# Mixer projections: step-size columns multiplied together with the gate columns, and the column copy divided between two engines

## What is computed

```python
cut = np.cumsum(IN_SPLITS)[:-1].tolist()   # pool, z, xbc, dt (12), qkv (1152), gate (384), a (12), b (12)
pc = jnp.split(h_ctx @ w_in, cut, axis=-1)
pl = jnp.split(h_lat @ w_in, cut, axis=-1)
s_lat, _, _ = ssd_stream(pl[1], pl[2], pl[3], *ssd_p, ssd_sf, ssd_sb)
g_lat, _, _ = gdn_stream(to_column_major(pl[4]), to_column_major(pl[5]), to_column_major(pl[6]),
                         to_column_major(pl[7]), *gdn_p, gdn_sf, gdn_sb)
# ssd_stream: dt = softplus(dt_raw + dt_bias);  gdn_stream: g = -exp(a_log) * softplus(a_raw + dt_bias), beta = sigmoid(b_raw)
```

## Time and profile before

| | |
|---|---|
| median of 3 runs | 4005.32 us (4003.27 to 4006.92) |
| span of the profiled execution | 4003.8 us |
| TensorE busy | 3512.2 us, 88% |
| VectorE, ScalarE, GpSimd busy | 47%, 27%, 31% |
| the stage in2 | from about 2418.7 to 2700 us of the span |

### The profile page before, as it was taken

How to read it: one execution, slowest core, us unless ns; L and a number is a source line. 1 busy time by engine, 2 the same in 40 slices (tenths; PEclk the granted TensorE clock), 3 DMA queues, 4 the chain that set the end, 5 groups by cost and what they waited for, 6 DMA issues and landing times. The chain is left out here.

```text
span 4003.8 us, 48185 instructions
## 1 busy us (share of the span) xinstructions
PE 3512.2 (88%) x16881; PEld 2311.3 (58%) x16881; DVE 1895.7 (47%) x4073; ACT 1088.2 (27%) x2218; POOL 1253.6 (31%) x1004
## 2 busy tenths in 40 slices
PE   8999997998898999999995898998867776949996
PEld 3745776676445667667565447574457764524442
DVE  2046662553663566766873450425479485240011
ACT  1023333442332232433442440221114112111111
POOL 2211010433333555655663452002212553211110
PEclk9999998999998999999998996998988877969998
DMA  4255532322541121112114423123325713347986
GB/s 133 92 165 143 163 120 79 107 84 101 203 148 32 58 65 56 46 55 65 52 43 156 163 111 84 42 71 104 115 78 157 255 51 125 119 173 253 325 313 230
DMA packets 417236, 494.07 MB, mean 123 GB/s; under 512 B 70786, under 2 KB 320922, under 8 KB 417011
## 3 DMA queue, kind: packets, MB, share of 16 engines
q1 hardware_dynamic: 391559, 463.71, 34.9%
q0 software_dynamic: 4608, 16.78, 1.6%
q10 hardware_dynamic: 20844, 10.68, 0.9%
HBM read 362.32 MB, written 128.77 MB: 123 GB/s over the span
## 5 line engine op out<-in xcount | busy, mean ns | idle before, releaser
L1067 POOL TENSOR_TENSOR hgrn_queries<-hgrn_qd,hgrn_pair_decay 128x640 f32<-128x640 f32 x192 | 263.2, 1390 | 293.3 <-PE hgrn_ps_a L1182 253.5
L1117 PE MATMUL hgrn_ps_w<-xT,hgrn_ring 128*128 128x512 f32 x432 | 196.0, 600 | 1.8 <-PEq L34 1.8
L396 PE MATMUL gla_bg_ps<-gla_bg_w,xT 128*128 128x256 f32 x768 | 186.0, 386 | 5.8 <-DMA gla_bg_w<-in_w_in_ab_dram 5.8
L530 POOL TENSOR_TENSOR l_wsum<-l_ring 128x512 f32<-128x512 f32 x14 | 20.0, 1430 | 507.9 <-PE att_bg_ps L562 187.2
L1721 PE MATMUL end_ps_z<-end_w,end_yT 128*128 128x512 f32 x384 | 166.9, 594 | 1.4 <-ACT end_yT L1668 1.4
L2843 PE MATMUL end_ps_z<-end_w,end_yT 128*128 128x512 f32 x384 | 167.3, 595 | 0.8 <-ACT end_yT L2771 0.8
L396 PEld LDWEIGHTS gla_bg_ps<-gla_bg_w,xT 128*128 128x128 f32 x768 | 144.4, 193 | 36.5 <-issue 10.6
L1287 DVE TENSOR_TENSOR hgrn_k_end<-hgrn_kd,hgrn_end_decay 128x128 f32<-128x128 f32 x168 | 136.0, 848 | 9.0 <-issue 2.2
L1117 PEld LDWEIGHTS hgrn_ps_w<-xT,hgrn_ring 128*128 128x128 f32 x432 | 81.6, 193 | 94.1 <-issue 93.8
L1117 PE MATMUL hgrn_ps_w<-hgrn_xs,hgrn_wsum 128*128 128x512 f32 x288 | 130.5, 601 | 4.6 <-ACT hgrn_sig L1401 4.6
L2162 ACT ACTIVATE att_s_sb<-att_s_sb,att_shift 128x256 f32<-128x256 f32 (+1 forms) x192 | 88.9, 464 | 166.3 <-DVE att_shift L2119 166.2
(11 more groups left out here) (681 smaller groups left out, 7861.5 us busy)
## 6 DMA issues: line engine op xcount, KB each, us to landing
expw_wg<-in_exp_w_gate_dram SPq DMA_DIRECT2D x16, 2048.0 KB, 10.1
expw_wu<-in_exp_w_up_dram SPq DMA_DIRECT2D x16, 2048.0 KB, 16.3
expw_wd<-in_exp_w_down_dram SPq DMA_DIRECT2D x16, 2048.0 KB, 21.9
att_w_ada<-in_ada_w_dram SPq DMA_DIRECT2D x24, 1024.0 KB, 6.8
hgrn_ring<-in_w_in_c_dram SPq DMA_DIRECT2D x18, 1024.0 KB, 5.4
l_ring<-in_w_in_ab_dram SPq DMA_DIRECT2D x14, 1024.0 KB, 5.7
end_gt<-gate_l SPq DMA_DIRECT2D x16, 768.0 KB, 8.6
hgrn_ring<-in_w_in_c_dram SPq DMA_DIRECT2D x24, 512.0 KB, 5.6
```

Of the source, the lines that this page charges most:

```text
L396: last = pe.matmul(bank[0:job.rows, q * job.width:(q + 1) * job.width], job.acts[:, k, t * P:t * P + job.rows], w[:, k, 0:job.width], star ...
L1067: pool.tensor_tensor(queries[:, d, s, :].rearrange("p (b a c) -> p b a c", b=POINTS, a=PC), q, f, ALU.mult).then_inc(queries_done, 1)
L1117: last = pe.matmul(bank[:, :], a[:, k, :], x(k), start=(fresh and k == 0), stop=(k == HK - 1), skip_group_check=True)
```

## The change

The 12 step-size columns lose their own two jobs. A `Job` can now have a second piece of columns `beside` the first, with a weight column and a destination of its own; the two pieces lie side by side in the weight buffer, are multiplied as one width, and are loaded and stored by a DMA each. On the context the step sizes stand beside the 24 columns a and b (width 36), on the latent tokens beside the 216 (width 228, on hT_cols). The lead-in has 5 fills for 7. The latent step sizes now lie in DRAM in column order of the tokens, and `Decays.load` reads them back into raster order, by two DMAs for the latent tokens and one for the context. The waits on loads and stores count the DMAs of the pieces. Of the eight column copies VectorE makes the first five, ahead of its clearing of in_u, and GpSimd the last three.

```diff
-    def __init__(self, kind, acts, tokens, weights, col, width, units, dst):
+    def __init__(self, kind, acts, tokens, weights, col, width, units, dst, beside=None):
         self.kind, self.acts, self.tokens, self.weights = kind, acts, tokens, weights
+        self.pieces = [(0, col, width, dst)]
+        if beside is not None:
+            self.pieces.append((width, *beside))
+            width += beside[1]
...
+        pieces = [len(job.pieces) for job, _ in self.units]
+        self.loads_by = [16 * sum(pieces[u % ring:u + 1:ring]) for u in range(len(self.units))]
+        self.stores_by = [16 * sum(pieces[self.fills[e][0]] for e in range(f % stages, f + 1, stages)) for f in range(len(self.fills))]
...
-        at = job.col + c * job.width
-        sp.dma_start(self.w[u % self.ring][:, :, 0:job.width],
-                     job.weights.rearrange("(k p) n -> p k n", p=P)[:, :, at:at + job.width]).then_inc(self.w_loaded[u % self.ring], 16)
+        for first, col, width, _ in job.pieces:
+            at = col + c * width
+            sp.dma_start(self.w[u % self.ring][:, :, first:first + width],
+                         job.weights.rearrange("(k p) n -> p k n", p=P)[:, :, at:at + width]).then_inc(self.w_loaded[u % self.ring], 16)
...
+            for first, _, width, dst in job.pieces:
+                out = dst[top:top + tall, c * width:(c + 1) * width].rearrange("(q p) c -> p q c", p=job.rows)
+                sp.dma_start(out, rows[:, :, first:first + width]).then_inc(self.stored[f % self.stages], 16)
...
-                    pe.wait_ge(self.w_loaded[u % self.ring], 16 * (u // self.ring + 1))
+                    pe.wait_ge(self.w_loaded[u % self.ring], self.loads_by[u])
...
-            wait(act, self.stored[f % self.stages], 16 * (f // self.stages))
+            wait(act, self.stored[f % self.stages], self.stored_of(f - self.stages))
...
-            sp.dma_start(self.raw[:, :, 0:H], self.dt_raw.rearrange("(t p) c -> p t c", p=P)).then_inc(self.loaded, 16)
+            lat = self.dt_raw[0:SEQ, :].rearrange("(w t b) c -> b w t c", t=TILES, b=2)
+            for b in range(2):
+                sp.dma_start(self.raw[b * GRID_W:(b + 1) * GRID_W, 0:TILES, 0:H], lat[b]).then_inc(self.loaded, 16)
+            sp.dma_start(self.raw[:, TILES:T2, 0:H], self.dt_raw[SEQ:ROWS2, :].rearrange("(t p) c -> p t c", p=P)).then_inc(self.loaded, 16)
...
-        dve.wait_ge(self.loaded, 112)
+        dve.wait_ge(self.loaded, 144)
...
+        BY_DVE = 5
...
+        def turn_columns(eng, k):
+            eng.tensor_copy(by_columns[:, k, :].rearrange("p (w r) -> p r w", r=GRID_H),
+                            by_rows[:, k, :].rearrange("p (r w) -> p r w", w=GRID_W)).then_inc(in_columns, 1)
+
         @block.gpsimd
         def _(pool):
-            for k in range(KB):
-                pool.tensor_copy(by_columns[:, k, :].rearrange("p (w r) -> p r w", r=GRID_H),
-                                 by_rows[:, k, :].rearrange("p (r w) -> p r w", w=GRID_W)).then_inc(in_columns, 1)
+            for k in range(BY_DVE, KB):
+                turn_columns(pool, k)
...
         def _(dve):
+            for k in range(BY_DVE):
+                turn_columns(dve, k)
             conv.clear(dve)
...
-                        Job(TOKEN, hcT, CTX, w, dt_at, DT_WIDTH, 1, dt_raw[con, :]),
-                        Job(TOKEN, hcT, CTX, w, ab_at, 2 * DT_WIDTH, 1, gate_ab[con, Z_WIDTH:GATE_AB]),
-                        Job(TOKEN, hT, SEQ, w, dt_at, DT_WIDTH, 1, dt_raw[lat, :]),
-                        Job(TOKEN, hT_cols, SEQ, w, gate_at + first, GATE_AB - first, 1, gate_ab[lat, first:GATE_AB]),
+                        Job(TOKEN, hcT, CTX, w, ab_at, 2 * DT_WIDTH, 1, gate_ab[con, Z_WIDTH:GATE_AB], (dt_at, DT_WIDTH, dt_raw[con, :])),
+                        Job(TOKEN, hT_cols, SEQ, w, gate_at + first, GATE_AB - first, 1, gate_ab[lat, first:GATE_AB], (dt_at, DT_WIDTH, dt_raw[lat, :])),
```

More of the change, by code:

```diff
@@ L349, in store @@
         else:
-            first, tall = n * job.per * job.rows, job.per * job.rows
-            out = job.dst[first:first + tall, c * job.width:(c + 1) * job.width].rearrange("(q p) c -> p q c", p=job.rows)
-            sp.dma_start(out, src[0:job.rows, 0:job.per * job.width].rearrange("p (q c) -> p q c", c=job.width)).then_inc(self.stored[f % self.stages], 16)
+            top, tall = n * job.per * job.rows, job.per * job.rows
+            rows = src[0:job.rows, 0:job.per * job.width].rearrange("p (q c) -> p q c", c=job.width)
+            for first, _, width, dst in job.pieces:
+                out = dst[top:top + tall, c * width:(c + 1) * width].rearrange("(q p) c -> p q c", p=job.rows)
+                sp.dma_start(out, rows[:, :, first:first + width]).then_inc(self.stored[f % self.stages], 16)
     def begin(self, sp):
@@ L375, in end, with stored_of, all_stored @@
             self.transfer(sp, g)
-        for b in range(self.stages):
-            sp.wait_ge(self.stored[b], 16 * len(range(b, len(self.fills), self.stages)))
+        self.all_stored(sp, len(self.fills))
+    def stored_of(self, f):
+        return 0 if f < 0 else self.stores_by[f]
+    def all_stored(self, sp, fills):
+        for f in range(max(0, fills - self.stages), fills):
+            sp.wait_ge(self.stored[f % self.stages], self.stored_of(f))
     def multiply(self, pe, g):
@@ L3093, in sigmoid @@
     def sigmoid(self, act):
-        act.wait_ge(self.loaded, 112)
+        act.wait_ge(self.loaded, 144)
         act.activation(self.beta[:, :, :], self.b_raw[:, :, :], ACT.Sigmoid)
@@ L3169, in _ @@
             bg.put(sp, LEAD + 1)
-            for b in range(bg.stages):
-                sp.wait_ge(bg.stored[b], 16 * len(range(b, LEAD, bg.stages)))
+            bg.all_stored(sp, LEAD)
             decays.load(sp)
```

## The result

In the first comparison the changed kernel took 3972.5 us (median of four runs, 3967.8 to 3983.3), the kernel before 4006.1 (four runs, 4003.3 to 4020.6). The ratio measured is 0.9901, with a 95% interval from 0.9876 to 0.9927; it is not the quotient of these two medians, which is 0.9916. Five more rounds of both kernels give 0.9921, from 0.9908 to 0.9935. The profiled execution of the changed kernel has a span of 3966.0 us for 4003.8. To tell what the change itself brought, the stage is read first.

A forecast was written before the change was run, and what follows sets the result against it. TensorE, 88% busy, was taken to bound the kernel. The lead-in sums to 1.0 + 6.8 + 1.3 + 26.7 = 35.8 us for 65.7, saving 29.9: span 3973.9, median 3975.4 us, range 3970 to 3984.5.

The forecast's parts named there:

- Steps 1 and 2: Lead-in: 160 narrow records removed, 34.1 us; the kept context fill, 36 columns wide, takes 6.8 us.
- Step 3: Lead-in start: the first fill needs two loads, so TensorE starts 1.0 us later (0.6 to 1.3).
- Step 4: Wide fills at 228 columns: 192.6 ns a record, 24.7 us, plus half the low-clock time; 26.7 us (26.2 to 27.2).
- Step 5: Column copies, five on VectorE and three on GpSimd, one after the other: TensorE waits 1.3 us (0 to 6.0).
- Steps 6 to 8: Lead-in: wide-fill weights hidden by 2 us, in_w by 17 us; extra stores and later decay loads cost nothing.
- Sum: Lead-in 35.8 us for 65.7, saving 29.9; everything behind moves with it; median 3975.4 us, bounds 3973.2 to 3980.9.
- Chances: Forecast and its bounds 0.80; faster 0.94, same 0.04, slower 0.02; range 3970 to 3984.5 us, including the spread of the runs.
- A: Rival: clock rises already in the narrow work, wide fills start at 2.4 GHz; 3.4 us more saved, 3972.0 us; chance 0.06.
- B: Rival: weights of the wide fills become the bound, TensorE waits 10 us; 21.0 us saved, 3984.3 us; chance 0.08.
- C: Rival: a later wait takes nearly all of the lead-in's gain, total within 0.2%; chance 0.04.
- D: Rival: late decay loads of latent step sizes delay ScalarE's sigmoid and stop TensorE; slower than before; chance 0.02.

The follow-up runs named there:

- the parts alone: Against the kernel before: only the context step sizes merged, copies shared, stage 62.2 us for 68.0; only the latent step sizes merged, 41.9 us.

## Why the prediction was right and where it was wrong

**Steps 1 and 2 (removed, context fill).** Right: 213 ns a record at 36 columns, and the parts alone brought 5.8 and 26.1 us.

**Step 3 (later start).** 1.0 us forecast; 3.36 us behind the first issue for 2.34: 1.0.

**Step 4 (wide fills).** 192.6 ns a record forecast, 192.5 seen. The time at low clock was set at 4 us from 3.0 to 4.9. The two traces of the changed kernel have 3.0 and about 5.3 us, the one with all copies on GpSimd about 4.4, and the one with the context fill last 5.7. The middle was right, the upper bound a little short.

**Step 5 (copies).** The mechanism was right, the size was off. The engines do take turns, and VectorE's copies were held as the row with 1.76 us had it. But the price of a copy was 0.91 us and not the 1.2 us that I took with its gap. The nearest row, a strided copy of the same shape at 1130 ns, was a tenth longer than the 1014 ns seen here, and in a row the copies have no gap but overlap by some 0.1 us. The copies ended 10.1 us behind the start for 11.4, and the wait was 0 for 1.3 us; that they ended 0.06 us ahead of TensorE is luck, since nothing in the sum made the two meet. The page "SBUF — State Buffer" of the Trainium skill (section "SBUF: two separate sides") has an exclusive lock on a shared port pair, held for a whole instruction. The shared copies agree with it: VectorE's copies beside GpSimd's were 2.62 to 2.75 us from start to start, for 1.77 + 0.91 = 2.68. The Trainium skill's page "VectorE: DVE Perf Modes" (section "Mode 2×_2P") has two elements a cycle for such a copy, by my estimate some 0.6 us. The runs do not show that: 0.91 us a copy is, by an estimate with the 0.96 GHz that this page of the Trainium skill gives, 1.2 elements a cycle.

**Steps 6 to 8.** Nothing waited for the weights of the wide fills, for stores or for the loads of the decays. The weights' two pieces landed at 2422.8 and 2423.4, 2.9 us before TensorE came to them, where 2 us were forecast. The last load of the decays was issued at 2463.1 and ScalarE's sigmoid came at 2488.8.

**The sum.** 29.9 us forecast for the stage, 31.8 and 30.7 seen in two traces of the changed kernel. Of the difference 1.3 us are step 5; the low clock of step 4 took 0.5 us less than forecast in the first trace and 0.6 us more in the second.

**The range.** This failed, and with it the forecast of the total. By the ratio of the first comparison the kernel is at 3965.7 us, 4.3 under the lower end of the range and 9.7 under the forecast of 3975.4. The stage accounts for 1.9 of these 9.7 us, and 3973.5 us, with the stage as measured, would have lain in the range. The step that was wrong is the one that I took for nothing: in **Sum** and **Chances** everything outside the stage is held still but for the spread of three runs, 4003.3 to 4006.9, 3.6 us in all. What the runs showed in its place: later executions of the same kernel before went from 4003.3 to 4020.6 us, and the pieces that the change does not touch varied by 13 us ahead of the stage and 11 behind. A ratio of four runs against four then has an interval 20 us wide (0.9876 to 0.9927), and its middle lay 8 us below what the stage gives. So the forecast of the stage stands, and the range was too narrow below for what a comparison of few runs can show. That the first comparison fell low and not high is chance.

**The rivals.** A, the clock rising in the narrow work, did not happen in the changed kernel, in line with the 40.9 us of the earlier trace rows. Three more runs show TensorE busy without a gap with narrow records and its clock falling from 2.4 to 1.2 GHz all the same. The page "TensorE: Matmul & The Clock Gate" of the Trainium skill (section "Part 1: The HAM clock gate") has activity release the gate; by these runs, a busy TensorE is not yet a reason to expect full clock. B did not happen, but its cover was thin: the weights landed 7.2 us behind the first issue, and in the run with two useless matmuls, with the same order of loads, 7.4 us behind it, 0.2 us before TensorE came to them. So a shorter way to the wide fills would have met B next. C and D left no mark: the first 163.3 us of the main loop are the same, and ScalarE read the decays' columns 25.7 us behind the last load's issue.

## What to carry to other kernels

When a stage opens with matmuls of few columns, read the granted clock beside the busy time: they cost a full weight load each, and in the low clock twice that, so columns of one weight matrix with the same tokens belong in one multiply even if their result must be put into another order afterwards. When the removed work was the cover of something, cost the thing that it covered first, here the column copies, and do not count on two engines copying side by side before a trace shows it. Add up a change by its own stage, and widen the range of the total by the spread of whole executions: three runs showed 3.6 us of it here, and later ones 17.

## What the runs showed of the hardware

- TensorE's granted clock fell from 1.00 to 0.50 while TensorE was busy without a gap, in narrow records (128-column weight loads with 12 or 36 streamed columns): 5.4 us behind the first of them in one run, 2.9 us in another, 3.4 us in a third, and not at all within 3.5 us in a fourth.
- VectorE and GpSimd, each with strided fp32 copies of 128x1024 in SBUF, took turns by instruction: 2.6 us from one VectorE copy to the next with GpSimd beside it, 0.91 us without. Another VectorE instruction, of two SBUF inputs, took 6.85 us once where its median is 0.56, while GpSimd ran eight instructions beside it; that GpSimd held it is not shown.
- Identical work ahead of the stage took between 2416.2 and 2429.3 us in thirteen executions. In the longest, an instruction that was 0.2 us behind came to be 3.0 us behind over 28 us, in which the clock was 0.57 for 1.00 in a stretch of 8 us.
